# A three-layer transformer kernel: loads of the beginning reordered, the last layer's gate products moved between its attention steps, and one weight load of the embedding stage started by an earlier event

## What is computed

```
h = x
for i in 0, 1:                                  # two layers
    h += mixer_i(rmsnorm(h))                    # 0: gated short convolution, 1: gated linear recurrence
    h += hier_moe(rmsnorm(h))                   # 32 experts, 2 per token, 3 weight matrices of 2 MB each
    h += sigmoid(rmsnorm(h) @ w_ple_gate + b) * (p[i] @ w_ple)     # "PLE"
h = rmsnorm(h)
# the attention layer, on xn = rmsnorm(h)
q, k, v, gates, z_n, z_d, index q/k = split(xn @ w_in)
o_cmp = attention over 31 compressed key blocks  # keys and values from a small MLP
o_sel = attention over all blocks, o_win = attention in a causal window
o_dsa = attention over the 256 keys with the highest index score per token
mixed = concat((g0*o_cmp + g1*o_sel + g2*o_win) * silu(z_n), o_dsa * silu(z_d))
out = h + mixed @ w_out
```

## Time and profile before

| | |
|---|---|
| median of three runs | 2091.7 us (2091.2 to 2097.75) |
| the profiled execution | 2084.6 us, span 2082.8 us |
| PE busy | 1958.3 us, 94% of the span |
| DVE, ACT, POOL busy | 767.9, 419.0, 105.6 us |
| the chain that ended last | PE 81%, DVE 8%, DMA 6%, issue 2% |
| DMA | 512.79 MB, 246 GB/s over the span |

### The profile page before, as it was taken

The page is one execution under the profiler, slowest core; times in us unless marked ns, Lnnn a source line. Parts: engine busy times, 40 slices in busy tenths (PEclk is TensorE's granted clock), DMA queues, the critical chain, the costliest instruction groups (busy, mean ns, idle before and its releaser), DMA issues.

```text
span 2082.8 us, 21308 instructions
## 1 busy us (share of the span) xinstructions
PE 1958.3 (94%) x8286; PEld 965.7 (46%) x8286; DVE 767.9 (37%) x2018; ACT 419.0 (20%) x871; POOL 105.6 (5%) x128
## 2 busy tenths in 40 slices
PE   7999999999999799999899999999978899998997
PEld 3444554444444335444355444444424554644554
DVE  3111453221111143456354422121115448656674
ACT  2000010111110124167010111111103432113442
POOL 0000000000000010025200000000010000000000
PEclk9999989999999999999989999999989999996999
DMA  6177279999999981110639999999995212200000
GB/s 279 41 157 294 73 309 408 428 427 428 428 427 428 425 359 41 66 56 0 262 132 378 415 428 428 428 428 428 428 399 216 87 71 81 96 26 1 21 11 11
DMA packets 46323, 512.79 MB, mean 246 GB/s; under 512 B 5248, under 2 KB 5248, under 8 KB 17152
## 3 DMA queue, kind: packets, MB, share of 16 engines
q1 hardware_dynamic: 37760, 481.38, 56.7%
q0 software_dynamic: 8448, 29.89, 3.6%
HBM read 484.90 MB, written 26.35 MB: 245 GB/s over the span
## 4 chain that ended last, share of the span: by engine, by line
PE 81%; DVE 8%; DMA 6%; issue 2%; ACT 1%; POOL 1%; another core or an unknown queue 0%; SPq 0%; DVEq 0%; POOLq 0%
PE ps L926 20%; PE ps L965 9%; PE ps L468 8%; PE ps L899 7%; PE ps L564 5%; PE ps L1317 5%; PE ps L1765 5%; DMA ring<-in_wexp 4%; PE ps L1480 4%; PE ps L2083 3%; PE ps L1511 3%; PE ps L1964 2%; PE ps L990 1%; PE ps L2101 1%; PE ps L2127 1%
## 5 line engine op out<-in xcount | busy, mean ns | idle before, releaser
L926 PE MATMUL ps<-ring,arena 128*48 128x512 f32 x1568 | 405.5, 607 | 39.8 <-issue 29.5
L926 PEld LDWEIGHTS ps<-ring,arena 128*48 128x48 f32 x1568 | 120.8, 125 | 241.9 <-issue 240.7
L939 DVE TENSOR_TENSOR arena<-arena,ps 48x512 f32<-48x512 f32 x64 | 44.1, 690 | 463.0 <-ACT arena L933 462.8
L965 PE MATMUL ps<-ring,arena 128*48 128x512 f32 x800 | 182.5, 596 | 3.4 <-ACT arena L953 2.8
L899 PEld LDWEIGHTS ps<-arena,h 128*128 128x128 f32 x1024 | 158.6, 190 | 44.6 <-issue 44.6
L899 PE MATMUL ps<-arena,h 128*128 128x192 f32 (+1 forms) x1024 | 174.3, 325 | 0.0
L468 PE MATMUL ps<-arena,ring 128*128 128x512 f32 x384 | 165.0, 592 | 1.0 <-DVE arena L305 1.0
L926 PE MATMUL ps<-arena 128*48 128x512 f32 x480 | 158.9, 610 | 1.0 <-issue 1.0
L1765 PE MATMUL ps<-ring,arena 128*128 128x512 f32 (+3 forms) x384 | 133.9, 503 | 0.0
L933 ACT ACTIVATE arena<-ps 48x512 f32<-48x512 f32 x64 | 37.9, 592 | 476.9 <-PE ps L926 463.8
L564 PE MATMUL ps<-ring,arena 128*128 128x512 f32 x256 | 114.8, 601 | 9.8 <-DMA ring<-in_wall 6.5
(11 more groups left out here) (278 smaller groups left out, 2117.8 us busy)
## 6 DMA issues: line engine op xcount, KB each, us to landing
ring<-in_wexp SPq DMA_DIRECT2D x148, 2048.0 KB, 19.5
arena<-in_wexp SPq DMA_DIRECT2D x44, 2048.0 KB, 21.8
ring<-in_wall SPq DMA_DIRECT2D x28, 2048.0 KB, 8.0
y_d<-arena POOLq DMA_DIRECT2D x60, 192.0 KB, 7.1
yo_d<-arena SPq DMA_DIRECT2D x2, 4032.0 KB, 41.9
xs_d<-h POOLq DMA_DIRECT2D x8, 512.0 KB, 3.8
ring<-in_wall SPq DMA_DIRECT2D x2, 1536.0 KB, 6.4
h<-in_x SPq DMA_DIRECT2D x4, 512.0 KB, 9.6
```

What stands on the lines that cost most here:

```text
L926: mm = pe.matmul(outs[m], xeT[:, e_ // 4 % 2, k, e_ % 4 * CAP:(e_ % 4 + 1) * CAP], ws[m][:, k, :], start=(k == 0), stop=(k == KT - 1))
L939: dve.tensor_tensor(hh[0:CAP, e_ % 2, :], sl[0:CAP, e_ % 2, :], banks[1][64:64 + CAP, :], ALU.mult).then_inc(S["hh"], 1)
L965: mm = pe.matmul(outs[c], hT_of(e_ % 2)[:, k, :], w[:, k, c * 512:(c + 1) * 512], start=(k == 0), stop=(k == 3))
```

## The change

Four parts.

1. **Loads of the beginning.** The identity is loaded by itself, right behind row tile 0 of x, under a semaphore of its own (`ident`); the other 2597 of the 2725 columns of `cst` are loaded behind the second ring unit, ahead of the third.
2. **The first product by row tile.** Column block 0 of the mixer is computed as four products over 128 tokens each (32 matmuls over 128 columns in place of 8 over 512); the first stands ahead of the last row tile's transposes.
3. **PLE's weights.** SP waits for `yg_1` in place of `yg_3`, loads the first unit in two halves, and POOL's gathers of row tiles 2 and 3 (and the bias load behind them) wait for the first half (`ple_a`).
4. **Attention's middle.** Only four z products stay in `pe_z`; the other four follow steps 0, 1, 4 and 7 of the core (`Z_AFTER`). They use bank 7; ACT copies three of them out raw, and applies silu to them in one instruction at the last. Topk's steps are spread anew: 20 and 9 at the waits for `pe_compress`, then 2, 3 and 4, and five in core steps 1, 2, 5 and 7. In the core ACT alone copies the turned probabilities; for row tiles 2 and 3 in one instruction over both banks, which is why `ps45` is one tensor now.

The diff, cut to what the prediction speaks of:

```diff
@@ -374,9 +378,10 @@
 
 
         def sp_start(sp):
+            a, b = OFF["ident"]
             sp.dma_start(h[:, 0, :], t_["x"][0:P, :]).then_inc(S["x0"], 16)
+            sp.dma_start(cst[:, a:b], t_["cst"][:, a:b]).then_inc(S["ident"], 16)
             sp.dma_start(gbuf[:, 0, :], t_["rows"][0:1, :].broadcast_to([P, D])).then_inc(S["g0"], 16)
-            sp.dma_start(cst[:], t_["cst"]).then_inc(S["cst"], 16)
             for i in range(1, NT):
                 sp.dma_start(h[:, i, :], t_["x"][i * P:(i + 1) * P, :]).then_inc(S[f"x{i}"], 16)
...
         def pe_first_norm(pe):
-            pe.wait_ge(S["cst"], 16)
-            for i in range(NT):
-                pe_trans(pe, 0, i)
+
+            def product(i):
+                pe_xT(pe, 0, i)
+                for k in range(KT):
+                    mm = pe.matmul(banks[0][:, i * P:(i + 1) * P], w8(("a", 0, 0))[:, k, 0:P], xT[:, k, i * P:(i + 1) * P], start=(k == 0), stop=(k == KT - 1))
+                if i == NT - 1:
+                    mm.then_inc(S["a_mm"], 1)
+
+            pe.wait_ge(S["ident"], 16)
+            pe_trans(pe, 0, 0)
+            pe_trans(pe, 0, 1)
+            pe_trans(pe, 0, 2)
+            pe_unit(pe, ("a", 0, 0))
+            product(0)
+            pe_trans(pe, 0, 3)
+            for i in range(1, NT):
+                product(i)
 
...
@@ -447,17 +466,18 @@
             for q in range(2):
                 for m in range(3):
                     sp_load(sp, ("a", q, m))
+                    if (q, m) == (0, 1):
+                        b = OFF["ident"][1]
+                        sp.dma_start(cst[:, b:], t_["cst"][:, b:]).then_inc(S["cst"], 16)
             sp.wait_ge(S["zrow"], 1)
             for l in range(2):
                 sp.dma_start(yo_d[l].rearrange("(s b) (z d) -> s (b z) d", b=NOVF, z=2),
                              zrow[0:CAP, :].unsqueeze(1).broadcast_to([CAP, 2 * NOVF, 512])).then_inc(S["cy"], 16)
 
         def pe_mixer_a(pe):
-            for i in range(NT):
-                pe_xT(pe, 0, i)
             for c in range(8):
                 q, c4 = divmod(c, 4)
-                for m in range(3):
+                for m in range(1 if c == 0 else 0, 3):
...
@@ -1123,6 +1144,8 @@
             pool.wait_ge(*M("ys_0", l, 16 * (NE - 2) // 2))
             pool.wait_ge(*M("ys_1", l, 16 * (NE - 2) // 2))
             for i in range(NT):
+                if i == 2:
+                    pool.wait_ge(*M("ple_a", l, 16))
                 for r in range(2):
...
         def sp_ple(sp, l):
-            sp.wait_ge(*M("yg_3", l, 16))
-            sp_load(sp, ("ple", l, 0))
+            sp.wait_ge(*M("yg_1", l, 16))
+            u = units[("ple", l, 0)]
+            for name, v in u.before:
+                sp.wait_ge(S[name], v)
+            half = UNIT // 2
+            sp.dma_start(u.ap[:, 0:half], u.src[:, 0:half]).then_inc(S["ple_a"], 16)
+            sp.dma_start(u.ap[:, half:], u.src[:, half:]).then_inc(S[f"ring{u.slot}"], 16)
             sp.wait_ge(*M("yg_7", l, 16))
             sp_load(sp, ("ple", l, 1))
...
+        Z_AFTER = {0: 4, 1: 5, 4: 6, 7: 7}
+
+        def pe_z_product(pe, m):
+            c, c4 = divmod(m, 4)
+            w = w8(("z", c))
+            if c4 == 0:
+                pe_unit(pe, ("z", c))
+            if m == 4:
+                pe.wait_ge(S["sd_cV"], 1)
+            elif m > 4:
+                pe.wait_ge(S["at_z"], m)
+            for k in range(KT):
+                mm = pe.matmul(banks[m if m < 4 else 7][:], w[:, k, c4 * P:(c4 + 1) * P], xT[:, k, :], start=(k == 0), stop=(k == KT - 1))
+            mm.then_inc(S["z_mm"], 1)
+
         def pe_z(pe):
-            for m in range(KT):
...
-                w = w8(("z", c))
-                if c4 == 0:
-                    pe_unit(pe, ("z", c))
-                if m >= 4:
-                    pe.wait_ge(S["at_z"], m - 3)
-                for k in range(KT):
-                    mm = pe.matmul(banks[m % 4][:], w[:, k, c4 * P:(c4 + 1) * P], xT[:, k, :], start=(k == 0), stop=(k == KT - 1))
-                mm.then_inc(S["z_mm"], 1)
+            pe_compress(pe, 0)
+            pe.wait_ge(S["at_pr"], 4 * GNO["v"] + NT)
+            pe.wait_ge(S["at_qk"], qk_through(len(BATCH) - 1))
+            pe_z_product(pe, 0)
+            pe_compress(pe, 1)
+            pe_compressed(pe, 0)
+            pe_z_product(pe, 1)
+            pe_compressed(pe, 1)
+            pe_z_product(pe, 2)
+            pe.wait_ge(S["sd_kro"], 1)
+            for g in range(2):
+                mm = pe.transpose(banks[6][:, 128 + 31 * g:159 + 31 * g], kro[0:31, g * P:(g + 1) * P], ident[0:31, 0:31])
+            mm.then_inc(S["sd_kt"], 1)
+            pe_z_product(pe, 3)
...
         def act_z(act):
-            for m in range(KT):
+            for m in range(4):
...
-                act.wait_ge(S["z_mm"], m + 1)
-                act.activation(ZT[:, m, :], banks[m % 4][:], ACT.Silu).then_inc(S["at_z"], 1)
-                if m == 3:
+                if m == 1:
                     act.wait_ge(S["at_ss"], 13)
                     act.activation(ssq[0:31, 0:2], ssq[0:31, 0:2], ACT.Sqrt).then_inc(S["at_rt"], 1)
+                act.wait_ge(S["z_mm"], m + 1)
+                act.activation(ZT[:, m, :], banks[m][:], ACT.Silu).then_inc(S["at_z"], 1)
+
+        def act_z_late(act, m):
+
+            if m == 7:
+                act.wait_ge(S["at_z"], 7)
+                act.activation(ZT[:, 4:7, :], ZT[:, 4:7, :], ACT.Silu)
+            act.wait_ge(S["z_mm"], m + 1)
+            act.activation(ZT[:, m, :], banks[7][:], ACT.Silu if m == 7 else ACT.Copy).then_inc(S["at_z"], 1)
...
-            some(16)
             for kv in range(2):
+                some(9 if kv else 20)
                 dve.wait_ge(S["sd_h"], kv + 1)
...
-                some(4)
...
+            some(2)
             dve.wait_ge(S["sd_o"], 2)
...
             o.then_inc(S["sd_cV"], 1)
+            some(3)
             dve.wait_ge(S["sd_kt"], 1)
             dve.tensor_copy(ar(Wk + 768, 62), banks[6][:, 128:190]).then_inc(S["sd_cT"], 1)
-            for _ in topk:
-                pass
+            some(4)
...
+            if k >= 2 or k == 1 and not one_bank(k):
+                pe.wait_ge(S["co_ev"], k - 1 if one_bank(k) and one_bank(k - 1) else k)
...
+                if s in Z_AFTER:
+                    pe_z_product(pe, Z_AFTER[s])
...
+                    act.wait_ge(S["co_t"], k + 1)
+                    if kind == "cmp":
+                        if i >= 1:
                             act.wait_ge(S["co_pv"], pairs(k_of("sel", i - 1, 3)))
-                        elif kind != "cmp" and k >= 2:
+                        o = act.activation(PTc.rearrange("p g c -> p (g c)"), banks[4 + k % 2][:, 0:2 * P], ACT.Copy)
+                    else:
+                        if k >= 2:
                             act.wait_ge(S["co_pv"], pairs(k - 2))
-                        if kind == "cmp":
-                            pt = PTc.rearrange("p g c -> p (g c)")
-                        width = 2 * P if kind == "cmp" else 2 * (i + 1) * P if one_bank(k) else (i + 1) * P
-                        act.activation(pt[:, 0:width], banks[4 if not one_bank(k) else 4 + k % 2][:, 0:width], ACT.Copy).then_inc(S["co_ea"], 1)
+                        width = (i + 1) * P
+                        if one_bank(k):
+                            o = act.activation(PT[:, k % 2, :, :].rearrange("p a s -> p (a s)")[:, 0:2 * width], banks[4 + k % 2][:, 0:2 * width], ACT.Copy)
+                        else:
+                            o = act.activation(PT[:, k % 2, :, 0:width], ps45[:].rearrange("p (a s) -> p a s", a=2)[:, :, 0:width], ACT.Copy)
+                    o.then_inc(S["co_ev"], 1)
...
-                if 0 <= s - 2 < NSU:
-                    k = s - 2
-                    kind, i, p = UN[SU[k]]
-                    pt = PT[:, k % 2, :, :].rearrange("p a s -> p (a s)")
-                    if not one_bank(k) or not (kind == "cmp" or k % 2 == 0):
-                        dve.wait_ge(S["co_t"], k + 1)
-                        if k >= 2:
-                            dve.wait_ge(S["co_pv"], pairs(k - 2))
-                        if one_bank(k):
-                            dve.tensor_copy(pt[:, 0:2 * (i + 1) * P], banks[4 + k % 2][:, 0:2 * (i + 1) * P]).then_inc(S["co_ed"], 1)
-                        else:
-                            dve.tensor_copy(pt[:, 512:512 + (i + 1) * P], banks[5][:, 0:(i + 1) * P]).then_inc(S["co_ed"], 1)
                 for n in step_units(s)[1:]:
                     dve_out_unit(dve, n)
+                for _ in range({1: 2, 2: 1, 5: 1, 7: 1}.get(s, 0)):
+                    next(topk, None)
+            assert next(topk, 1) == 1
```

More of the change, by code:

```diff
@@ L2048, in one_bank @@
             return kind == "cmp" or i <= 1
-        def by_act(k):
-            return sum(1 for q in range(k + 1) if not one_bank(q) or UN[SU[q]][0] == "cmp" or q % 2 == 0)
-        def by_dve(k):
```

(3 more changed lines are left out.)

57 lines of the change are left out of this document (22 added, 35 removed).

## The result

The changed kernel takes 2069.4 us in the median of 4 runs (2062.0 to 2071.7), the kernel before 2094.7 us in 4 runs taken beside it (2091.2 to 2099.5): a ratio of 0.987, 95% interval 0.985 to 0.990. 2066 us was forecast.

A forecast was written before the change was run, and what follows sets the result against it. A chain over PE was taken to bound the kernel, except each MoE's DMA-bound second half. Gains 4.0 + 2.1 + 0 + 15.3 + 4.0 = 25.4 us took 2084.6 to 2059.2, plus 7.1 gave 2066 us; range 2055 to 2082.

The forecast's parts named there:

- The beginning: First transposes and first product: constants out of the way, product ends earlier; gain 4.0 us, between 1.2 and 4.7, all kept.
- The sign that I had named against it: MoE: the prediction would be wrong if the weight stream ends at the same time as before.
- rival A': The DMA-bound MoE swallows the beginning's gain; kernel at 2070 us, chance 0.05.
- The second PLE: PE's 3.8 us wait for weights could go, but the bias comes late; net gain 2.1 us, bounds +3.8 and -2.7.
- The first PLE: PE waited only 0.31 us there, so nothing to win; 0 taken, bounds +0.3 and -4.
- rival C: Bias late in both PLEs, -2.7 and -4 in place of +2.1; kernel at 2075 us, chance 0.11.
- Attention's middle: Z products spread among the core's first steps; 13.2 us earlier and output product 2.1 us shorter: 15.3 us, bounds 2 and 17.
- products 6 and 7 at full speed: Attention's middle: these z products take 6.96 us each, behind core steps 2 to 4 (5.5 us) and 5 to 7 (5.4).
- Steps 8 to 12 at full clock: Attention's core: 1.38 us each by DVE, with ACT's change of function 1.7; 8.5 us in all, to 1891.3.
- rival B: Clock falls in the core's idle places, products 6 and 7 start slow; middle gains 2, kernel at 2079 us, chance 0.20.
- The rest: Rest of attention's core: DVE loses its copies, for which PE waited 3.7 us; gain 4 us, between 0 and 8.
- The level: Whole kernel: median of the runs stands 7.1 us above the profiled execution, so 2059.2 becomes 2066 us.

The follow-up runs named there:

- e7: Changed kernel with the turned weights copied as before, DVE taking its part again; 2074.1 us, ratio to the kernel before 0.9903.
- e4: Changed kernel plus 33 needless PE matmuls where PE waited for DVE in core steps 3 to 12; ratio to the kernel before 0.9863.
- b1: The kernel before, unchanged, profiled once more; 2091.7 us.
- b2: The kernel before, unchanged, profiled once more for the spread; 2094.2 us.
- e5: Changed kernel plus 16 needless PE matmuls where PE waited for DVE in core steps 3 to 12; ratio to the kernel before 0.9842.
- e3: The kernel before with only the attention part of the change; ratio to the kernel before 0.9933.
- e6: Changed kernel without POOL's wait for the first half of PLE's weights; ratio to the kernel before 0.9905.
- e9: Changed kernel plus six needless PE matmuls in the beginning; ratio to the kernel before 0.9866.
- e8: Changed kernel with the core's five topk steps moved to its steps 0 and 1; 2059.0 us, ratio to the kernel before 0.9824.
- e2: The kernel before with only the part on PLE's weights; ratio to the kernel before 0.9939.
- e10: Changed kernel with the edits of e8 and e9 and seven needless matmuls in the core; ratio to the kernel before 0.9833.

## Why the prediction was right, and where it was wrong

The total was right, 2069.4 against 2066 us, and in part by luck. Against the forecast's 25.4 us, the ledger has the middle 9.8 us short and the other terms 6.3 us over (3.5 and 1.9 in the two PLEs, 0.4 and 0.5 in the beginning and the rest). That makes 21.9 us; the medians show 25.3, and the last 3.4 us are in no column.

- **The beginning, 4.0 us: right in size, with wrong details.** Measured 4.4. The transposes start at 9.0 to 10.5 us and not at 8.5, since the small load of the identity stands ahead of the gain row; the product ends at 25.4 (e7) to 28.0 us (e4), but the old order's usually ends later too than the 29.2 us that I read. The gain is kept: the norm of row tile 0 in the first PLE starts at 747.9 us in the mean of the seven kernels with the new beginning and at 753.7 in the five with the old, 5.8 us earlier. The sign that I had named against it, the MoE's weight stream at the same time as before, does show in the two first profiles (at 476.99 us both start the same down product, L965 and L986); but in b1 and b2 that product starts at 479.23 and 479.46 us, so it was the lucky start of the first, not rival A'.
- **The second PLE, 2.1 us: right in mechanism, too small.** Measured 4.0. DVE waits 2.68 us for the bias (1.7 forecast), which landed after 7.15 us (7.5 estimated). The wait that goes is 4.6 to 4.9 us in b1 and b2, not 3.80, and the product behind it takes 8.6 to 9.3 us there.
- **The first PLE, 0: wrong, 3.5 us.** The failed step is "in the first PLE PE waited 0.31 us only, so there is nothing to win". b1 and b2 show 2.33 and 2.99 us; the profile's 0.31 was short because a late copy of ACT had held PE up just ahead. The bias is late there by 0.87 us in the changed kernel and 0.47 in e5, which rival C had at 4.
- **Attention's middle, 15.3 us: wrong, 5.5.** The steps up to product 5 came as forecast (first scores at 1839.3, which is 1842.5 in the time of the first profile, for 1842.2; product 5 over at 1858.4 for 1857.9). The failed step is products 6 and 7 at full speed, 6.96 us each, behind steps of 5.5 and 5.4 us: in the four profiles of this code the products take 8.1 to 9.7 us, and the steps ahead of them 6.0 to 6.7. "Steps 8 to 12 at full clock" failed in the changed kernel's profile alone (19.3 us from product 7 to the output product; 15.8 in e3, e6 and e9, 15.5 forecast). I counted 5 us of waiting in steps 2 to 7, which is what came (5.3), and put rival B at 0.20 because "these gaps are shorter, and products stand between": 2.11 and 1.81 us were enough. e5 shows it by filling the waits (6.2 us of the missing 10 come back), and e8 agrees by removing them (7.9), though there DVE's work moves too.
- **The rest, 4.0 us: right.** Measured 4.5, and e7 shows that all of it is the copies.
- **The level: "the median is 7.1 us above" was carried over as an offset.** It was right for the sum, but I did not ask what those 7 us were. They were stages on which the argument rested: 2.5 us at the start, and the first PLE.
- **Two slips that move nothing:** the lower end of the beginning is 4.7 - 3.4 = 1.3 us and not 1.2, and the second tile's transposes start at 14.51 us in the trace, not at 14.46.

On transposes and the clock the prediction weighed the Trainium skill ("TensorE: Matmul & The Clock Gate", Part 4: PE-mode transpose). The rule says that transposes do not count as work that raises the clock; the runs leave it open. In e3 the clock came up while nothing but transposes had run, against the rule (timeline of PE):

```profile
14.54 1.97 PE L298 MATMUL ps<-cst,arena 128*128 128x128 f32 x8 [2.44 <-DVE arena L279]
17.02 1.77 PE L298 MATMUL ps<-cst,arena 128*128 128x128 f32 x8 [0.51 <-DVE arena L279]
19.50 1.09 PE L298 MATMUL ps<-cst,arena 128*128 128x128 f32 x8 [0.71 <-DVE arena L279]
```

The first profile of before agrees: its last eight transposes take 1.83 us and the product behind them is at full speed. In b1, b2 and e2 the clock did not come up until the product, and in e10 it fell among transposes, 1.4 us apart, as the rule would have it; but waits stood there too, and no run here separates the two.

## What to carry to other kernels

A wait of 2 us in front of a long product costs more than 2 us when the clock falls in it (here 1.0 to 2.6 us more in each of the two products), so when products are spread over a serial chain, first take the other engine's extra work out of the steps around them, and put it beside the products, where that engine idles. A small wait in a profile proves a stage free only if nothing unusual stands just ahead of it: profile the kernel twice before a term is set to zero. When a load must be early, look at what else is on the DMA engines: here issuing it sooner won only with other DMAs held back.

## What the hardware showed unasked

- The same code takes different times stage by stage: 201.8 to 204.4 us to the end of the first mixer, where the kernels with the longest time (b1, b2, e2) are those whose first product starts at the lower level, and 20.1 to 26.4 us for the old first PLE, by PE's wait and the clock behind it, while 162.2 us of the old core's later part repeat to 0.1 us.
- A 128 x 256 matmul of this data type stands as two records and takes 0.46 us at 2.4 GHz (9 in 4.15 us in e4); I had counted half.
- With a load of 64 KB ahead of it the gain row lands 5.9 to 7.4 us after its issue (nine profiles), without it 5.1 to 5.3 (five).
